# Second layer's experts: u and v rows in one table, one 8 KB gather per token and slot, weighted sum by a diagonal tile

## Chip, core and metric

The kernel runs on one core of a Trainium2 chip. The metric is the device time of one execution in microseconds (us), as the median of three runs. A core has a matrix engine (PE), a vector engine (DVE), a scalar engine (ACT), a general engine (POOL, GpSimd), which also writes the descriptors of indirect transfers, a queue engine (SP) for plain transfers, and 16 DMA engines that all transfers share.

## The reference

Two layers, each a token mixer followed by a feed-forward part with 16,384 small experts. Only the feed-forward part of the second layer is touched. It works on 256 tokens of width 1024, in two tiles of 128. For each token and each of 8 heads it picks 16 experts and adds their outputs:

```
q = (xb @ w_q).reshape(T, PEER_HEADS, 2, PEER_DQ // 2)
s = jnp.einsum('thpd,hpnd->thpn', q, keys).astype(jnp.float32)
s_top, i_top = lax.top_k(s, PEER_TOPK)
...
best, sel = lax.top_k(cand, PEER_TOPK)
eidx = jnp.take_along_axis(cidx, sel, axis=-1)
g = jax.nn.softmax(best, axis=-1)
act = jax.nn.gelu(jnp.einsum('td,thkd->thk', xb, u[eidx]).astype(jnp.float32))
return jnp.einsum('thk,thkd->td', (g * act).astype(v.dtype), v[eidx]).astype(h.dtype)
```

So each of the 256 tokens needs 128 rows of `u` and the same 128 rows of `v`, 4 KB each in fp32: 128 MB of `u` and 128 MB of `v` in all (268 million bytes). Nothing of it is reused, since every token has its own list. I call one pair (expert number 16h+k of each token of a tile) a slot: a tile has 128 slots, the layer 256.

## The kernel before

After the first layer and the second layer's mixer, `phase_norm` leaves the normed tokens in `hT` (a token per partition) and transposed in `hp`. Then `phase_stream` (L1817) does all of the experts' part, with a hand-written order on every engine and semaphores between them:

- **Scores.** PE runs 16 queries (`query`, L1972, 24 products of 128x256 each at L117 to L119, then `sub_scores`, L1927). ACT splits each weight slab in a high part (`w_hi`, L2011), DVE in a low part (`low`, L2101), and ACT copies query and scores out of PSUM (L2023, L2008).
- **Routing.** DVE runs `route` (L2080) once per tile and head, 16 times: the top 16 of both halves, of their sums, and the expert numbers, a chain of short instructions in which each waits for the one before.
- **u rows.** POOL gathers one row of `in_u_rows` per token for each slot (L1922, 128 rows of 4 KB, 512 KB in all). DVE multiplies it with `hT` and sums (`dot`, L2125, at L2132).
- **Weights.** After 64 slots of a tile (a unit `u`, 4 in all), ACT takes Exp and Gelu of 64 columns at once (L2034, L2039), DVE multiplies with the gates (`weights`), PE transposes expert numbers and weights (L1941, L1946), and DVE spreads the weights into `wdiag`, whose columns are mostly zero (`spread_weights`, L2149).
- **v rows.** Here a gather takes the 64 rows of each of two tokens (the transposed numbers `eidT`). Four such gathers make a `quad` (L1948): 8 products of 128x512 whose weights have 32 columns, four in each half going to four different groups of 32 output rows. So a quad reads 2 MB.

POOL's order is a list (`order`, L1836): the 64 `u` gathers of the first unit, then 4 `u` and 4 `v` gathers by turns, then 64 `v` gathers. All go through a ring of 18 buffers of 4 KB per partition; a gather waits until its buffer was consumed (`consumed`, L1854), by a dot or by a quad. DVE alternates in pieces of a head: a whole `route`, then the 16 dots of the head before, with up to three `low` between them. At the end `evac`, `turn_back` and `add_back` bring the sum of each tile back to `xT`, and `phase_norm` and one store end the program. The first layer's experts (`phase_mixed`) use gathers of 4 KB rows too, beside plain loads of the same tables by SP.

## Time and profile before

| | us |
|---|---|
| median of 3 runs (3319.77 to 3323.53) | 3321.89 |
| span of the profiled execution, first to last instruction | 3310.8 |
| outside the span, against the median | 11.1 |
| first gather of `phase_stream` issued | 2490.5 |
| last one issued | 3281.6 |
| last quad ends | 3289.2 |
| DVE's share of the span | 62% |
| PE's share of the span | 70% |

The profiled execution has no time of its own beside its span. The clock of PE that the hardware granted (PEclk in the views) is given as a share of 2.4 GHz: 1.00 is 2.4 GHz, 0.50 is 1.2 GHz, and a value between is a mean over a stretch with both. "DMA share" is the mean busy share of the 16 DMA engines, GB/s what they moved. A matmul in fp32 leaves two records; records that lie side by side are merged in the timeline, which gives the time from the first start to the last end.

### The profile page before, as it was taken

How to read it: one execution, taken by the hardware profiler on the slowest of the kernel's cores; microseconds unless marked ns; L12 is line 12 of the kernel's file. 1: busy time of each engine (PE TensorE's matmuls, PEld its weight loads, DVE VectorE, ACT ScalarE, POOL GpSimd, SP SyncE). 2: the span in 40 equal slices, each digit the busy share in tenths (PEclk: the TensorE clock that was granted, in tenths of full speed). 3: DMA queues.
4: the chain of work that ended last, by engine and by line, in shares of the span. 5: the costliest groups of instructions: out<-in, count | busy, mean ns of one | idle time of the engine just before them, and what ended most of it. 6: DMA issues, size and time to landing. Idle time of an engine off the chain costs nothing. (4 is left out here: it accounts for less than half of the span.)

```text
span 3310.8 us, 41079 instructions
## 1 busy us (share of the span) xinstructions
PE 2319.7 (70%) x15570; PEld 1772.9 (54%) x15570; DVE 2038.1 (62%) x4539; ACT 884.6 (27%) x1475; POOL 1445.0 (44%) x1270
## 2 busy tenths in 40 slices
PE   5977799794558787888899998887973423333345
PEld 3777555592357777777678775786553300000001
DVE  3576444499968898888543344665537956656530
ACT  3323144321363333333233333422431100000000
POOL 1034001330017675565655552022046677767764
PEclk8975698896789999999899999886876756565566
DMA  5210141134359999999999996210037799999997
GB/s 204 67 29 1 59 153 52 64 129 152 127 212 406 407 404 365 400 390 400 402 405 406 405 406 264 93 30 9 1 110 280 267 358 356 349 363 349 353 374 269
DMA packets 248756, 816.92 MB, mean 247 GB/s; under 512 B 26776, under 2 KB 45784, under 8 KB 247664
## 3 DMA queue, kind: packets, MB, share of 16 engines
q0 software_dynamic: 147456, 536.94, 42.3%
q1 hardware_dynamic: 101104, 277.35, 22.4%
q8 instruction: 125, 2.05, 0.3%
q14 instruction: 71, 0.58, 0.1%
HBM read 796.37 MB, written 17.83 MB: 246 GB/s over the span
## 5 line engine op out<-in xcount | busy, mean ns | idle before, releaser
L1960 PE MATMUL ps<-sparse_ring,sparse_wdiag 128*32 128x512 f32 x1024 | 225.7, 995 | 402.2 <-DMA sparse_ring<-in_v_rows,eidT 372.7
L2322 POOL DMA_INDIRECT sparse_ring<-in_v_rows,eidT x256 | 282.7, 1104 | 291.8 <-PE ps L2371 220.8
L2132 DVE CUSTOM_DVE_ANT_0 sparse_ring<-sparse_ring,hT 128x1024 f32<-128x1024 f32 x256 | 304.7, 1222 | 163.5 <-DMA sparse_ring<-in_u_rows,eid 159.2
L2322 POOL DMA_INDIRECT sparse_ring<-in_u_rows,eid x256 | 347.1, 1356 | 118.0 <-issue 68.1
L117 PE MATMUL ps<-h_hi,peer_uh 128*128 128x256 f32 x1024 | 310.3, 303 | 83.6 <-DVE peer_ul L2434 77.3
L1960 PEld LDWEIGHTS ps<-sparse_ring,sparse_wdiag 128*32 128x32 f32 x1024 | 44.4, 152 | 573.0 <-issue 573.0
L1922 POOL DMA_INDIRECT sparse_ring<-in_u_rows,eid x256 | 299.4, 1169 | 102.7 <-issue 75.9
L1922 POOL DMA_INDIRECT sparse_ring<-in_v_rows,eidT x256 | 280.8, 1097 | 123.4 <-issue 73.7
L2460 DVE CUSTOM_DVE_ANT_0 sparse_ring<-sparse_ring,hT 128x1024 f32<-128x1024 f32 x256 | 304.1, 1223 | 37.1 <-DMA sparse_ring<-in_u_rows,eid 34.9
L119 PE MATMUL ps<-h_hi,peer_ul 128*128 128x256 f32 x1024 | 299.0, 292 | 1.9 <-issue 1.9
L118 PE MATMUL ps<-h_lo,peer_uh 128*128 128x256 f32 x1024 | 299.6, 293 | 0.5 <-issue 0.4
L118 PE MATMUL ps<-peer_wl,peer_vh 128*128 128x256 f32 x1024 | 290.8, 284 | 2.6 <-issue 2.6
L119 PE MATMUL ps<-peer_wh,peer_vl 128*128 128x256 f32 x1024 | 290.4, 284 | 2.0 <-issue 1.9
L117 PE MATMUL ps<-peer_wh,peer_vh 128*128 128x256 f32 x1024 | 291.4, 285 | 0.3 <-issue 0.3
L117 PEld LDWEIGHTS ps<-h_hi,peer_uh 128*128 128x128 f32 x1024 | 206.1, 201 | 149.1 <-DVE peer_ul L2434 95.5
L2434 DVE TENSOR_TENSOR peer_ul<-peer_u,peer_uh 128x1024 fp32r<-128x1024 f32 x128 | 156.5, 1222 | 180.7 <-ACT peer_uh L2399 111.4
L2399 ACT ACTIVATE peer_uh<-peer_u 128x1024 fp32r<-128x1024 f32 x128 | 135.2, 1057 | 305.1 <-DMA peer_u<-in_uT 291.4
L119 PEld LDWEIGHTS ps<-h_hi,peer_ul 128*128 128x128 f32 x1024 | 206.2, 201 | 2.9 <-issue 2.9
L118 PEld LDWEIGHTS ps<-h_lo,peer_uh 128*128 128x128 f32 x1024 | 206.6, 202 | 0.8 <-issue 0.7
L117 PEld LDWEIGHTS ps<-peer_wh,peer_vh 128*128 128x128 f32 x1024 | 197.6, 193 | 4.7 <-issue 4.7
L119 PEld LDWEIGHTS ps<-peer_wh,peer_vl 128*128 128x128 f32 x1024 | 197.3, 193 | 2.9 <-issue 2.9
L118 PEld LDWEIGHTS ps<-peer_wl,peer_vh 128*128 128x128 f32 x1024 | 197.4, 193 | 1.7 <-issue 1.6
(410 smaller groups left out, 5385.4 us busy)
## 6 DMA issues: line engine op xcount, KB each, us to landing
peer_u<-in_uT SPq DMA_DIRECT2D x128, 512.0 KB
peer_v<-in_v_rows SPq DMA_DIRECT2D x128, 512.0 KB
ada_slab<-in_ada_w SPq DMA_DIRECT2D x20, 2048.0 KB, 8.6
proj_slab<-in_w_fm SPq DMA_DIRECT2D x38, 512.0 KB
route_slab<-in_w_pq SPq DMA_DIRECT2D x32, 512.0 KB, 3.3
peer_gates<-dense_stage SPq DMA_DIRECT2D x4, 4096.0 KB, 13.0
peer_gates<-peer_gates SPq DMA_DIRECT2D x32, 512.0 KB
out_slab<-in_w_out SPq DMA_DIRECT2D x16, 512.0 KB, 3.8
```

Source lines behind the costliest of these rows:

```text
L117: nc.tensor.matmul(out, w[0], x[0], start=start, stop=False)
L118: nc.tensor.matmul(out, w[0], x[1], start=False, stop=False)
L119: return nc.tensor.matmul(out, w[1], x[0], start=False, stop=stop)
L1922: nc.gpsimd.indirect_dma_start(out=ring[:, s % R], out_offset=None, in_=rows, in_offset=bass.IndirectOffsetOnAxis(ap=col, axis=0)).then_in ...
L1960: mm = nc.tensor.matmul(ps[32 * q:32 * (q + 1), 6 + half, :], wdiag[:, q, HQ * half_h + j, :], ring[:, s % R, half * BANK:(half + 1) * BAN ...
L2132: nc.vector.tensor_tensor_reduce(out=ring[:, s % R], in0=ring[:, s % R], in1=hT[:, t], scale=1.0, scalar=0.0, op0=ALU.mult, op1=ALU.add, a ...
L2322: nc.gpsimd.indirect_dma_start(out=ring[:, s % R], out_offset=None, in_=rows, in_offset=bass.IndirectOffsetOnAxis(ap=at, axis=0)).then_inc ...
L2399: nc.scalar.activation(uh[:, e % 2], us[:, e % SW], ACT.Copy).then_inc(uhi, 1)
L2434: nc.vector.tensor_tensor(ul[:, e % 2], us[:, e % SW], f32(uh[:, e % 2]), ALU.subtract).then_inc(ulo, 1)
L2460: nc.vector.tensor_tensor_reduce(out=ring[:, s % R], in0=ring[:, s % R], in1=hT[:, t], scale=1.0, scalar=0.0, op0=ALU.mult, op1=ALU.add, a ...
```

## The change

The two layers' tables are no longer one. The first layer reads `peer_u[0]` and `peer_v[0]` as before; for the second a table `in_uv_rows` holds the `u` row and the `v` row of an expert side by side, 8 KB. In `phase_stream`:

- POOL issues 256 gathers of 128 rows of 8 KB in place of 512 of 4 KB. The ring has 11 buffers of 8 KB per partition (88 KB, before 72 KB), and a buffer is free when the slot's product is done.
- The weighted sum is made per slot: `slot` multiplies the `v` half of the buffer by a 128x128 diagonal tile with the slot's weights, two products of 128x512, all 256 slots into four banks (two per tile). The transposes, `eidT` and `wdiag` go.
- ACT makes the weights for two slots at a time (`weights`): a Gelu of 2 columns, two scalings by the gate, and two diagonal tiles out of `ident`, of which there are 4 buffers. Exp and sum of a head are one instruction, 16 in all, and the gates another.
- DVE runs `dot` per slot on the `u` half, with two steps of a `route` (of 14) after each until all are done; the queries 5 to 15 are spread over the first 33 slots on PE, ACT and DVE (`query_at`).

The diff, cut to its core (the routing's instructions are the same, cut into steps by `yield`):

```diff
-            R = 18
+            S = nt * NS
+            R = 11
+            DG = 4
+            FIRST = 5
+            query_at = {(2 * i + 1 if i < 3 else 3 * i - 1): FIRST + i for i in range(HP + 1 - FIRST)}
...
-                ring = sb(st, f"sparse_ring{l}", [P, R, D_MODEL])
+                ring = sb(st, f"pair_ring{l}", [P, R, 2 * D_MODEL])
+                diag = sb(st, f"pair_diag{l}", [P, DG, P])
...
+                        for s in range(S):
                             if s >= R:
-                                pool.wait_ge(*consumed(s - R))
+                                pool.wait_ge(slot_mm, s - R + 1)
+                            if s % TOPK == 0:
+                                pool.wait_ge(eid_done, s // TOPK + 1)
+                            nc.gpsimd.indirect_dma_start(out=ring[:, s % R], out_offset=None, in_=d["uv_rows"],
+                                                         in_offset=bass.IndirectOffsetOnAxis(ap=eid[:, s:s + 1], axis=0))\
+                                .then_inc(row_in[s % R], 16)
...
+                        def slot(s):
+                            t, i = s // NS, s % NS
+                            pe.wait_ge(diag_done, s + 1)
+                            for half in range(2):
+                                mm = nc.tensor.matmul(ps[:, 4 + 2 * t + half, :], diag[:, s % DG, :],
+                                                      ring[:, s % R, D_MODEL + half * BANK:D_MODEL + (half + 1) * BANK],
+                                                      start=(i == 0), stop=(i == NS - 1))
+                            mm.then_inc(slot_mm, 1)
...
+                        for c in range(FIRST):
                             query(c)
+                        for s in range(S):
+                            slot(s)
+                            if query_at.get(s, HP) < HP:
+                                query(query_at[s])
+                            elif s in query_at:
+                                sub_scores(HP - 1)
...
+                        def weights(s):
+                            act.wait_ge(dot_done, s + 2)
+                            nc.scalar.activation(dots[:, s:s + 2], dots[:, s:s + 2], ACT.Gelu_apprx_tanh).then_inc(gelu_done, 1)
+                            act.wait_ge(gelu_done, s // 2 + 1)
+                            if s % TOPK == 0:
+                                act.wait_ge(gate_done, s // TOPK + 1)
+                            for x in (s, s + 1):
+                                nc.scalar.activation(dots[:, x:x + 1], dots[:, x:x + 1], ACT.Copy, scale=gate[:, x:x + 1]).then_inc(wt_done, 1)
+                            for x in (s, s + 1):
+                                act.wait_ge(wt_done, x + 1)
+                                if x >= DG:
+                                    act.wait_ge(slot_mm, x - DG + 1)
+                                nc.scalar.activation(diag[:, x % DG], ident[:], ACT.Copy, scale=dots[:, x:x + 1]).then_inc(diag_done, 1)
...
+                        for s in range(S):
+                            dot(s)
+                            next(routes, None)
+                            next(routes, None)
+                            if query_at.get(s, HP) < HP:
+                                low(query_at[s])
+                            if s % TOPK == 11 and s + TOPK < S:
+                                invert(s // TOPK + 1)
+                            if s == NS + 24:
+                                add_back(0)
...
-    a["u_rows"] = peer_u.reshape(-1, D_MODEL)
-    a["v_rows"] = peer_v.reshape(-1, D_MODEL)
+    a["u_rows"] = peer_u[0]
+    a["v_rows"] = peer_v[0]
+    a["uv_rows"] = np.concatenate([peer_u[1], peer_v[1]], axis=-1)
```

How the instructions stand now. On DVE, before, from the end of the second head's `route` on (ISA is the dot and the read of its sum):

```order
L2095 SCALAR_TENSOR_TENSOR route_ij<-route_ij 128x16
L2098 TENSOR_SCALAR eidf<-route_ij 128x16
L2099 TENSOR_SCALAR eid<-route_ij 128x16
L2132 ISA sparse_ring,sparse_dots<-sparse_ring,hT 128x1024
L2132 ISA sparse_dots 128x1
L2132 ISA sparse_ring,sparse_dots<-sparse_ring,hT 128x1024
```

and after the change, from the first dot on (L2103 is the dot, L2098 is `low`, L2038 to L2088 the steps of `route`):

```order
L2103 ISA pair_ring,pair_dots<-pair_ring,hT 128x1024
L2103 ISA pair_dots 128x1
L2038 MAX route_top<-route_s 128x8 x2
L2042 MAX_INDEX route_idx<-route_top,route_s 128x8 x2
L2043 MATCH_REPLACE route_s<-route_top,route_s 128x128 x2
L2103 ISA pair_ring,pair_dots<-pair_ring,hT 128x1024
L2103 ISA pair_dots 128x1
L2047 MAX route_top<-route_s 128x8 x2
L2051 MAX_INDEX route_idx<-route_top,route_s 128x8 x2
L2052 TENSOR_TENSOR route_cand<-route_top 128x256
L2098 TENSOR_TENSOR route_wl<-route_slab,route_wh 128x1024
```

A dot now stands after every second step, where sixteen stood in a row after a whole `route`. On PE, at the end of the stream, before (L1960 is the quads, L1941 and L1946 the transposes, L1969 `turn_back`):

```order
L1960 MATMUL ps<-sparse_ring,sparse_wdiag 32x512 x112
L1941 MATMUL ps<-ident,eid_twice 128x128
L1960 MATMUL ps<-sparse_ring,sparse_wdiag 32x512 x8
L1946 MATMUL ps<-ident,sparse_wt_twice 128x128
L1960 MATMUL ps<-sparse_ring,sparse_wdiag 32x512 x136
```

and after (L1919 is `slot`, L1928 `turn_back`):

```order
L1895 MATMUL ps<-route_keys,route_q 128x128 x2
L1919 MATMUL ps<-pair_ring,pair_diag 128x512 x6
L1895 MATMUL ps<-route_keys,route_q 128x128 x2
L1919 MATMUL ps<-pair_ring,pair_diag 128x512 x216
L1928 MATMUL ps<-ident,hT 128x128 x8
L1919 MATMUL ps<-pair_ring,pair_diag 128x512 x230
```

There are 512 products in both, now 128 rows wide and not 32. On ACT, which had 8 instructions for the weights of all four units beside 8 table loads, the same stretch is now, around the fifth pair of slots (L1955 `w_hi`, L1963 and L1948 the copies out of PSUM, L1983 Gelu, L1988 scaling, L1993 diagonal tile, L1973 Exp):

```order
L1955 ACTIVATE route_wh<-route_slab 128x1024
L1963 ACTIVATE route_q<-ps 128x256
L1948 ACTIVATE route_s<-ps 128x256
L1983 ACTIVATE pair_dots<-pair_dots 128x2
L1988 ACTIVATE pair_dots<-pair_dots,gate 128x1 x2
L1993 ACTIVATE pair_diag<-ident,pair_dots 128x128 x2
L1973 ACT_TABLE_LOAD
L1973 ACTIVATE route_best,route_esum<-route_best,route_nbest 128x16
L1983 ACT_TABLE_LOAD
L1983 ACTIVATE pair_dots<-pair_dots 128x2
```

Five instructions stand between the dots of a pair and its products, and an Exp with two table loads comes once per 16 slots.

## Rows read from the trace of the kernel before

**Rows 1.** The windows view: busy time of each engine in nine stretches.
```profile
core 0: us, PE busy (x) PEld busy (x) DVE busy (x) ACT busy (x) POOL busy (x), PEclk, DMA share, GB/s
2478.00:2492.00 14.00, 6.68 (x52) 6.28 (x51) 11.11 (x38) 4.07 (x8) 1.49 (x1) 0.91 0.12 39
2492.00:2496.00 4.00, 4.00 (x20) 4.00 (x20) 0.49 (x1) 0.00 (x0) 3.08 (x4) 0.50 0.94 281
2496.00:2516.00 20.00, 4.43 (x37) 4.24 (x35) 5.18 (x26) 3.32 (x6) 11.28 (x13) 0.67 1.00 399
2500.00:2640.00 140.00, 53.34 (x318) 50.52 (x317) 126.62 (x318) 22.43 (x40) 96.40 (x67) 0.69 0.79 281
2640.00:3200.00 560.00, 176.34 (x782) 35.39 (x782) 323.93 (x782) 9.04 (x13) 422.25 (x381) 0.58 0.96 356
3205.00:3270.00 65.00, 37.71 (x184) 7.97 (x184) 0.00 (x0) 0.00 (x0) 43.54 (x47) 0.70 0.97 374
1400.00:1500.00 100.00, 81.70 (x631) 73.09 (x630) 80.60 (x121) 33.15 (x49) 60.83 (x49) 0.91 1.01 393
1750.00:1950.00 200.00, 195.81 (x1610) 156.84 (x1612) 80.13 (x102) 69.62 (x103) 109.20 (x101) 1.00 1.03 406
1300.00:1900.00 600.00, 539.02 (x4222) 451.18 (x4220) 368.36 (x528) 198.92 (x294) 352.41 (x302) 0.95 1.02 401
```

**Rows 2.** Groups by line with shapes kept apart, from 2400 us to the end.
```profile
L1922 POOL DMA_INDIRECT sparse_ring<-in_u_rows,eid x256 | 299.4, 1169 | 102.7 <-issue 75.9 <-DVE eid L2099 26.3 <-remote 0.3
L1922 POOL DMA_INDIRECT sparse_ring<-in_v_rows,eidT x256 | 280.8, 1097 | 123.4 <-issue 73.7 <-remote 28.0 <-DVE eidT L2139 12.9
L1960 PE MATMUL ps<-sparse_ring,sparse_wdiag 128*32 128x512 f32 x1024 | 225.7, 995 | 402.2 <-DMA sparse_ring<-in_v_rows,eidT 372.7 <-issue 29.5
```

**Rows 3.** Timeline of POOL: start us, us, engine, line, operation, idle before it.
```profile
2490.51 1.77 POOL L1922 DMA_INDIRECT sparse_ring<-in_u_rows,eid  x1 [14.27 <-DVE eid L2099]
2492.58 0.94 POOL L1922 DMA_INDIRECT sparse_ring<-in_u_rows,eid  x1 [0.30 <-issue]
...
2526.00 1.98 POOL L1922 DMA_INDIRECT sparse_ring<-in_u_rows,eid  x1 [0.30 <-issue]
2528.28 1.99 POOL L1922 DMA_INDIRECT sparse_ring<-in_u_rows,eid  x1 [0.30 <-issue]
...
2543.26 0.94 POOL L1922 DMA_INDIRECT sparse_ring<-in_u_rows,eid  x1 [0.30 <-issue]
2544.50 0.94 POOL L1922 DMA_INDIRECT sparse_ring<-in_u_rows,eid  x1 [0.30 <-issue]
```

**Rows 4.** Timeline of DVE in the first heads.
```profile
2521.37 1.22 DVE L2132 CUSTOM_DVE_ANT_0 sparse_ring<-sparse_ring,hT 128x1024 f32<-128x1024 f32 x1
2522.52 1.22 DVE L2132 CUSTOM_DVE_ANT_0 sparse_ring<-sparse_ring,hT 128x1024 f32<-128x1024 f32 x1
...
2540.82 0.48 DVE L2066 MAX8 route_top<-route_s 128x8 f32<-128x128 f32 x2
...
2549.47 1.22 DVE L2132 CUSTOM_DVE_ANT_0 sparse_ring<-sparse_ring,hT 128x1024 f32<-128x1024 f32 x1
```

**Rows 5.** Timeline of PE: two quads, then a square fp32 product with 512 columns.
```profile
3140.39 3.64 PE L1960 MATMUL ps<-sparse_ring,sparse_wdiag 128*32 128x512 f32 x16 [11.61 <-DMA sparse_ring<-in_v_rows,eidT]
...
3287.28 1.92 PE L1960 MATMUL ps<-sparse_ring,sparse_wdiag 128*32 128x512 f32 x16 [1.31 <-DMA sparse_ring<-in_v_rows,eidT]
...
27.65 1.88 PE L297 MATMUL ps<-hk,meanD 128*128 128x512 f32 x4
```

**Rows 6.** Timeline of PE in the first queries, and one product of scores.
```profile
2473.33 0.41 PE L119 MATMUL ps<-h_hi,route_wl 128*128 128x256 f32 x1
2473.54 0.41 PE L117 MATMUL ps<-h_hi,route_wh 128*128 128x256 f32 x1
...
2479.06 0.28 PE L119 MATMUL ps<-h_hi,route_wl 128*128 128x256 f32 x1
2479.18 0.28 PE L117 MATMUL ps<-h_hi,route_wh 128*128 128x256 f32 x1
...
2499.82 0.61 PE L1933 MATMUL ps<-route_keys,route_q 128*128 128x128 f32 x4
```

**Rows 7.** Groups of ACT in the whole program, shapes kept apart.
```profile
L1782 ACT ACTIVATE hot_j<-iota,dense_nj 128x128 f32<-128x128 f32 x102 | 31.5, 389 | 12.6 <-DVE dense_nj L1753 12.6
L943 ACT ACTIVATE scan_xq<-cum 128x128 f32<-128x128 f32 x15 | 3.6, 296 | 0.0
L2034 ACT ACT_TABLE_LOAD x4 | 5.1, 1283 | 0.1
L2015 ACT ACTIVATE route_wh<-route_slab 128x1024 fp32r<-128x1024 f32 x14 | 14.8, 1057 | 111.3 <-PE ps L119 89.4 <-issue 13.5 <-remote 8.4
L2023 ACT ACTIVATE route_q<-ps 128x256 f32<-128x256 f32 x16 | 5.9, 369 | 21.0 <-PE ps L119 21.0
L1136 ACT ACTIVATE lame<-lame 128x2 f32<-128x2 f32 x2 | 0.4, 204 | 10.6 <-DVE lame L1280 10.6
```

**Rows 8.** What L1922 and L1960 do: ns min/median/max, first and last start.
```profile
L1922 POOL DMA_INDIRECT sparse_ring<-in_u_rows,eid x256: 934/941/2007, 2490.5 to 3181.9; - x128
L1922 POOL DMA_INDIRECT sparse_ring<-in_v_rows,eidT x256: 932/941/1989, 2632.8 to 3281.6; - x128
...
L1960 PE MATMUL ps<-sparse_ring,sparse_wdiag x1024: 589/1061/1064, 2643.0 to 3288.6; 128*32 128x512 f32 x171
```
**Rows 9.** The waits view, 2640 to 3290: total us, times, longest.
```profile
PE ps L1960 <- DMA sparse_ring<-in_v_rows,eidT: 372.7, 56, 12.9
```

More of the change, by code:

```diff
@@ L21 @@
 from contextlib import ExitStack
+import itertools
 import math
@@ L1861, in phase_stream @@
+            (dot_done, gelu_done, wt_done, diag_done, slot_mm, acc_ev, tr_mm) = (
+                sem(f"stream_{x}{l}") for x in ("dot", "gelu", "wt", "diag", "slot_mm", "acc_ev", "tr_mm"))
             with ExitStack() as st:
@@ L2047, in _ @@
+                        queried(1)
+                        queried(2)
                         exps(0)
-                        gelu(0)
-                        exps(1)
-                        gelu(1)
-                        exps(2)
-                        gelu(2)
-                        evac(0)
-                        exps(3)
-                        gelu(3)
+                        queried(3)
+                        gates(0)
+                        queried(4)
+                        for s in range(0, S, 2):
+                            weights(s)
+                            for x in (s - 2, s - 1):
+                                if query_at.get(x, HP) < HP:
+                                    queried(query_at[x])
+                                elif x in query_at:
+                                    s_copy(HP - 1)
+                            if s % TOPK == 8 and s + TOPK < S:
+                                exps(s // TOPK + 1)
+                            if s % TOPK == 12 and s + TOPK < S:
+                                gates(s // TOPK + 1)
+                            if s == NS + 4:
+                                evac(0)
@@ L2125, in dot @@
-                        def dot(t, h, between=()):
-                            for i in range(TOPK * h, TOPK * (h + 1)):
-                                if i % TOPK in (5, 10, 15) and len(between) >= i % TOPK // 5:
-                                    low(between[i % TOPK // 5 - 1])
-                                s = at["u", t, i]
-                                dve.wait_ge(row_in[s % R], 16 * (s // R + 1))
-                                nc.vector.tensor_tensor_reduce(
-                                    out=ring[:, s % R], in0=ring[:, s % R], in1=hT[:, t], scale=1.0, scalar=0.0,
-                                    op0=ALU.mult, op1=ALU.add, accum_out=dots[:, t, i:i + 1]).then_inc(dot_done, 1)
@@ L2149, in spread_weights, with dot @@
-                        def spread_weights(u):
-                            dve.wait_ge(wt_mm, u + 1)
-                            dve.wait_ge(diag_cleared, 1)
-                            if u >= 2:
-                                dve.wait_ge(quad_mm, HQ * (u - 1))
-                            nc.vector.tensor_copy(diag(u % 2, 0), of_token(ps[:, 4, P:2 * P], 0))
-                            nc.vector.tensor_copy(diag(u % 2, 1), of_token(ps[:, 4, P:2 * P], 1)).then_inc(spread, 1)
+                        def dot(s):
+                            dve.wait_ge(row_in[s % R], 16 * (s // R + 1))
+                            row = ring[:, s % R, 0:D_MODEL]
+                            nc.vector.tensor_tensor_reduce(out=row, in0=row, in1=hT[:, s // NS], scale=1.0, scalar=0.0,
+                                                           op0=ALU.mult, op1=ALU.add, accum_out=dots[:, s:s + 1]).then_inc(dot_done, 1)
@@ L2194, in _ @@
-                        last = 2 * nt - 1
-                        dot(nt - 1, PH - 1)
-                        close(last)
-                        weights(last)
-                        add_back(0)
-                        spread_weights(last)
+                        low(2)
+                        for _ in route(0):
+                            pass
+                        low(3)
+                        low(4)
+                        invert(0)
+                        routes = itertools.chain.from_iterable(route(j) for j in range(1, nt * PH))
@@ new lines, in _ @@
+                        for s in range(S):
[8 more added lines that the diff above has]
+                                add_back(0)
+                        for _ in routes:
+                            pass
```

299 lines of the change are left out of this document (97 added, 202 removed).

## Prediction, made before the change was run

> **What bounds the kernel now.** I read the windows view first, then the groups by line, then timelines. The first layer is untouched, so only what runs from 2490.5 us on counts. From 2640 to 3200 the DMA engines look full: share 0.96, 356 GB/s [rows 1]. That tempts one to say that the stream is bound by memory, and that moving the same 268 MB in larger pieces changes nothing. Two other rows of the same view speak against it: the same gathers, alone, moved 399 GB/s from 2496 to 2516, when sixteen of them were issued in a row, and the first layer's stretch holds 401 GB/s for 600 us, two gathers in three transfers among it [rows 1].
>
> What is full is POOL. It was busy for 422.25 us of these 560, with 381 gathers: 1.11 us each. In front of each the timeline shows 0.30 us of idle time put down to "issue" [rows 3], so 381 x 1.41 = 537 us, 96% of the stretch. The timeline also tells why a gather costs 1.11: 0.94 us where DVE does short routing steps or nothing, 1.98 us where DVE runs its dots back to back [rows 3, 4]. At 2.29 us for 512 KB POOL feeds 229 GB/s, at 1.24 us 423 GB/s. I read the DMA share of 0.96 as packets that take longer because little is queued behind them. From 3205 to 3270, with DVE idle, the rate rises to 374 GB/s [rows 1].
>
> Before 2640 it is DVE that is full: 126.62 us of 140, at 281 GB/s [rows 1]. One head costs 30 us there: 8.65 us of `route` (from 2540.82 to 2549.47), 16 dots and up to 3 `low` at 1.15 us each [rows 4]. PE waits for its `v` rows most of the time: 402.2 us of idle time before L1960, 372.7 of it by DMA [rows 2].
>
> **The change, part by part.**
>
> POOL. 512 gathers become 256. If the cost is one per row descriptor, each still has 128 rows, so 0.94 to 1.99 us plus 0.30: 1.24 to 2.29 us per MB, where before it was 2.5 to 4.6. That is below every other term here. If a row of 8 KB costs two descriptors, it is twice 0.94 to 1.99 and one 0.30: with dots for 40% of the time, 2 x 1.36 + 0.30 = 3.0 us. No gather of 8 KB rows is in this trace. I take the first, the nearest row, and keep 3.0 as a rival.
>
> DMA. 1,048,576 bytes per slot. At 401 GB/s, the rate held over 600 us with two queues, this is 2.61 us; at 410 it would be 2.56, at 356, the rate of this stream now, 2.95. I take 2.61.
>
> PE. This is the price of the change. A quad has 8 products in four groups of 32 output columns that run side by side: its 16 records take 3.64 us at one time and 1.92 us at another [rows 5]. A slot has only 2 products, but 128 wide, so nothing runs beside them: the record pitch of the square product at L297 is (1.88 - 0.59)/3 = 0.43 us, 4 records 1.72 us [rows 5]; at half the clock 3.44 us. So a slot costs PE about what a quad does, and there are 256 instead of 64. In all 440 us at 2.4 GHz or 881 us at 1.2 GHz, for a stream that lasts some 680 us. The queries add 11 x (24 x 0.12 + 0.61) = 38 us [rows 6], at half the clock the 24 take 0.21 each.
>
> Which clock is granted? Now, with PE idle for two thirds of the stretch, 0.58; with 37.71 us busy of 65, 0.70; with 82 of 100 busy, 0.91; with 98% busy, 1.00 [rows 1]. In rows 6 the queries begin at 0.21 us each and go on at 0.12 without a gap between them. A slot needs 1.72 of 2.61 us at full clock, 66%, and more than all of it at half, so at the low clock PE never idles, and in rows 6 the work without idle time is what raised the clock. I expect a mean near 0.8, 2.15 us per slot. The Trainium skill warns of the contrary in "TensorE: Matmul & The Clock Gate", section "HAM oscillation — how this bites in real kernels": bursts of matmuls shorter than the wait for data between them start slow each time. What this would give is the third rival.
>
> DVE. Per slot a dot, 1.15, and two of 14 steps of a route, 2 x 8.65/14 = 1.24: 2.39 us, under 2.61. In the first 33 slots 11 `low` add 0.38. The routes end after 15 x 14/2 = 105 slots; from there it is 1.15 to 1.3. Steps that waited for their forerunner now have a dot in between.
>
> ACT. Per pair of slots a Gelu of 2 columns, two scalings, two tiles: 3 x 0.20 + 2 x 0.39 = 1.4 us (0.30 to 0.39 for a tile, by its two nearest rows) of 5.2 us [rows 7]. It is on no path by its sum, but it stands in each slot's. Behind it on ACT stand `w_hi`, 1.06, and the copies, 0.37, for which DVE's `low` and PE's query wait. 15 heads bring two table loads, 2 x 1.28, each: in front of a pair, and not in sum.
>
> The ring. A buffer is held from its issue until its product. I add: 2.1 for POOL at most, 5.7 from issue to landing (the last gather starts at 3281.6, the last quad at 3287.28 [rows 5, 8]), a dot that waits and one that runs, 3.6, the pair's partner, 2.6, ACT 1.4, PE up to 3.4: 19 us, with the table loads 21. Eleven buffers at 2.61 us are 28.7 us. The ring isn't the bound; at the low clock on PE it nearly is.
>
> **The sum.** The first gather starts when it did, at 2490.5: what comes ahead of it (five queries, the first route) is as before. The second has landed near 2500 (5.7 us after its issue, 1.3 for the larger size), a dot, 1.2, and ACT's Gelu, scalings and first tile with a table load, some 2.7 us, to 2504, follow, and PE can begin slot 0 at 2505. The first 33 slots: PE's own work is 33 x 1.72 + 38 = 95 us at full clock, DVE's 33 x 2.77 = 91 us, DMA's 86. These hold each other up (a query waits for `low`, `low` for `w_hi`, and that for the query two before), so I take PE's at a clock of 0.9: 106 us, to 2611. By then the ring is full, about 40 slots have landed, and 216 are to come: 216 x 2.61 = 564 us, to 3175. The last pair's dots, ACT and two slots on PE take 7 us: 3182. Before, the last quad ended at 3289.2, and what follows (`evac`, `turn_back`, `add_back`, final norm) is unchanged. That is 107 us less. I give back 8 us for dips in the DMA share at the table loads and `turn_back(0)`: 99 us less, a span of 3211.8. The median of the runs was 11.1 us above the span, so **3223 us**.
>
> **The rivals.**
>
> 1. *Memory is the bound already.* If rows taken at random cannot come faster than the 356 GB/s of now, a slot takes 2.95 us: 2611 + 216 x 2.95 + 7 = 3255, 34 us less, 3288. For it: the DMA share of 0.96. Against it: the 399 GB/s of the same gathers. The Trainium skill takes this side: "DMA: Bandwidth & Descriptors", section "Where 436 GB/s comes from", has about 358 GB/s for a core's share of HBM as what binds; this trace disagrees, with 401 GB/s over 600 us. Chance 0.12.
> 2. *POOL stays the bound.* Two descriptors for a row, 3.0 us per slot: 2611 + 648 + 7 = 3266, 23 us less, 3299. Chance 0.08.
> 3. *PE becomes the bound, and the kernel is slower.* If the clock stays at 1.2 GHz through the stream, as it mostly does now, the stream lasts 256 x 3.44 + 11 x (24 x 0.21 + 1.2) = 949 us from 2505 on, to 3454: 165 us more, 3487. It decides from the clock at which a slot takes more than 3.1 us, (3289 - 2611 - 7)/216, which is 0.55 of full. For it: 0.58 granted in the stream now. Against it: that is with 56 waits for DMA of up to 12.9 us [rows 9], and no row shows a PE without idle time that stayed slow. Chance 0.10.
> 4. *The chain per slot is longer than I add up*: a wait between POOL, DVE, ACT and PE in the first 33 slots costs 40 us more, or the ring runs short in the routes. About 3263. Chance 0.12.
>
> My forecast has 0.58.
>
> **How the numbers follow.** The likeliest case by itself reaches from 3200 (410 GB/s and no dips: 107 + 11 less, 3204; a little for a faster start) to 3250. The range takes in rivals 1, 2 and 4, so 3195 to 3300, and leaves out rival 3 and what lies beyond it. A measurement of this kernel tells 0.2% from no change, 6.6 us. Faster by more than that: the forecast and rivals 1, 2 and 4, less a little for mixed cases, 0.87. Within it 0.03, slower 0.10.
>
> **What would show it.** Right: gathers near or above 400 GB/s after slot 33, POOL idle for a third of the time or more with about 256 spans of 1 to 2 us, PEclk above 0.75 in the stream, and idle time of PE before its slots put down to ACT's tile, and of ACT's Gelu to dots that wait for DMA. The first 33 slots would end near 2611. Wrong: PE busy for over 95% with PEclk near 0.5 (rival 3), POOL's spans above 2.2 us on average (rival 2), a DMA share of 1 at 360 GB/s with POOL idle (rival 1), or gathers that wait for PE's `slot_mm` while the DMA engines are below 0.9 (rival 4).

## The result, and the profile after

The changed kernel takes **3185.05 us** (median of four runs, 3183.18 to 3187.82) where the kernel before takes 3320.83 on the same chip (four runs, 3309.5 to 3323.53): a ratio of 0.9600, 95% interval 0.9583 to 0.9618. The prediction had 3223 us with a range from 3195 to 3300: right in direction, but the range did not hold the result, which lies 10 us under its lower end. The profiled execution has a span of 3181.7 us and a time of 3183.49; its span is 129.1 us shorter than that of before.

The windows view of the kernel after, its columns as in [rows 1]:

```profile
2496.00:2516.00 20.00, 8.47 (x45) 6.73 (x44) 8.01 (x28) 5.95 (x13) 7.38 (x8) 0.67 1.01 422
2520.00:2540.00 20.00, 20.00 (x103) 13.83 (x102) 17.49 (x51) 9.88 (x27) 6.36 (x7) 1.00 1.01 417
2580.00:2600.00 20.00, 18.07 (x79) 11.74 (x79) 13.92 (x40) 9.10 (x25) 8.96 (x6) 0.91 0.94 380
2600.00:2640.00 40.00, 39.28 (x115) 19.11 (x114) 39.53 (x126) 16.82 (x57) 26.16 (x21) 1.00 0.97 384
2640.00:3120.00 480.00, 358.66 (x776) 139.85 (x774) 293.95 (x667) 159.92 (x540) 189.66 (x193) 0.99 1.01 421
```

The DMA engines, at 281 GB/s up to 2640 and 356 from there on before [rows 1], now move 417 to 422 GB/s but for one dip around 2600, where PE is busy for 18.07 of 20 us and then for 39.28 of 40. POOL is busy for 40% of the long stretch, PE for 75% of it, at a granted clock of 0.99.

The groups by line, as in [rows 2]:

```profile
L1919 PE MATMUL ps<-pair_ring,pair_diag 128*128 128x512 f32 x1024 | 476.3, 610 | 144.8 <-ACT pair_diag L1993 142.2 <-issue 2.6
L2103 DVE CUSTOM_DVE_ANT_0 pair_ring<-pair_ring,hT 128x1024 f32<-128x1024 f32 x256 | 312.9, 1222 | 206.7 <-DMA pair_ring<-in_uv_rows,eid 206.7
L1883 POOL DMA_INDIRECT pair_ring<-in_uv_rows,eid x256 | 268.2, 1048 | 391.9 <-PE ps L1919 364.0 <-DVE eid L2088 17.8 <-issue 10.2
L1993 ACT ACTIVATE pair_diag<-ident,pair_dots 128x128 f32<-128x128 f32 x256 | 87.4, 387 | 2.0 <-PE ps L1919 1.7
```

Read the third row against POOL's two in [rows 2]: 512 gathers and 580 us have become 256 and 268, and the idle time in front of a gather is no longer "issue" but a wait for PE, which frees the buffer. A gather of 8 KB rows costs POOL what one of 4 KB rows costs, 0.94 us with little beside it. PE waits for ACT's diagonal tiles, ACT for the dots, and DVE's dots for landings. So the transfers bind, and each engine waits for them in its turn.

The timeline of POOL where the ring first fills, and in the middle of the stream (columns as in [rows 3]):

```profile
2502.10 0.94 POOL L1883 DMA_INDIRECT pair_ring<-in_uv_rows,eid  x1 [0.30 <-issue]
2503.34 0.94 POOL L1883 DMA_INDIRECT pair_ring<-in_uv_rows,eid  x1 [0.30 <-issue]
...
2804.45 0.94 POOL L1883 DMA_INDIRECT pair_ring<-in_uv_rows,eid  x1 [0.78 <-PE ps L1919]
2807.70 0.94 POOL L1883 DMA_INDIRECT pair_ring<-in_uv_rows,eid  x1 [2.31 <-PE ps L1919]
```

and DVE's, there, a dot every 2.49 us:

```profile
2815.54 1.22 DVE L2103 CUSTOM_DVE_ANT_0 pair_ring<-pair_ring,hT 128x1024 f32<-128x1024 f32 x1 [1.25 <-DMA pair_ring<-in_uv_rows,eid]
2816.69 0.08 DVE L2103 DVE_READ_ACCUMULATOR2_ANT pair_dots<- 128x1 f32 x1
2818.03 1.23 DVE L2103 CUSTOM_DVE_ANT_0 pair_ring<-pair_ring,hT 128x1024 f32<-128x1024 f32 x1 [1.26 <-DMA pair_ring<-in_uv_rows,eid]
```

I paired the k-th gather with the k-th dot over the whole stream. From slot 60 on, a dot begins some 20 us after POOL was done with its gather (17.8 to 21.1): eight transfers of 2.49 us stand in front of it. This *lead* of POOL over the dots tells most of what follows.

### The profile page after: what moved, and what is told of

Its sections match the earlier page's. It is cut to its first block and busy times, and to the rows that moved or that the text cites. A ratio compares the mean times of both kernels' runs of the same rounds, so it can differ in the third digit from the quotient of the medians.

```text
span 3181.7 us, 41584 instructions
## 1 busy us (share of the span) xinstructions
PE 2546.1 (80%) x15562; PEld 1903.4 (60%) x15562; DVE 2022.4 (64%) x4495; ACT 1084.4 (34%) x2179; POOL 1119.1 (35%) x1013
## 5 line engine op out<-in xcount | busy, mean ns | idle before, releaser
L1919 PE MATMUL ps<-pair_ring,pair_diag 128*128 128x512 f32 x1024 | 476.3, 610 | 144.8 <-ACT pair_diag L1993 142.2
L2103 DVE CUSTOM_DVE_ANT_0 pair_ring<-pair_ring,hT 128x1024 f32<-128x1024 f32 x256 | 312.9, 1222 | 206.7 <-DMA pair_ring<-in_uv_rows,eid 206.7
L1919 PEld LDWEIGHTS ps<-pair_ring,pair_diag 128*128 128x128 f32 x1024 | 187.1, 192 | 423.3 <-ACT pair_diag L1993 228.5
L1883 POOL DMA_INDIRECT pair_ring<-in_uv_rows,eid x256 | 268.2, 1048 | 391.9 <-PE ps L1919 364.0
L2251 POOL DMA_INDIRECT sparse_ring<-in_v_rows,eidT x256 | 279.5, 1092 | 298.4 <-PE ps L2300 226.9
L2251 POOL DMA_INDIRECT sparse_ring<-in_u_rows,eid x256 | 339.4, 1326 | 122.5 <-issue 68.1
L2389 DVE CUSTOM_DVE_ANT_0 sparse_ring<-sparse_ring,hT 128x1024 f32<-128x1024 f32 x256 | 304.7, 1224 | 41.9 <-DMA sparse_ring<-in_u_rows,eid 35.7
L2300 PE MATMUL ps<-sparse_ring,sparse_wdiag 128*32 128x512 f32 x1024 | 137.2, 653 | 67.2 <-DMA sparse_ring<-in_v_rows,eidT 66.2
```

What stands on the lines that cost most here:

```text
L1883: nc.gpsimd.indirect_dma_start(out=ring[:, s % R], out_offset=None, in_=d["uv_rows"], in_offset=bass.IndirectOffsetOnAxis(ap=eid[:, s:s + ...
L1919: mm = nc.tensor.matmul(ps[:, 4 + 2 * t + half, :], diag[:, s % DG, :], ring[:, s % R, D_MODEL + half * BANK:D_MODEL + (half + 1) * BANK], ...
L2103: nc.vector.tensor_tensor_reduce(out=row, in0=row, in1=hT[:, s // NS], scale=1.0, scalar=0.0, op0=ALU.mult, op1=ALU.add, accum_out=dots[:, ...
L2251: nc.gpsimd.indirect_dma_start(out=ring[:, s % R], out_offset=None, in_=rows, in_offset=bass.IndirectOffsetOnAxis(ap=at, axis=0)).then_inc ...
L2300: mm = nc.tensor.matmul(ps[32 * q:32 * (q + 1), 6 + half, :], wdiag[:, q, j, :], ring[:, s % R, half * BANK:(half + 1) * BANK], start=(j = ...
L2389: nc.vector.tensor_tensor_reduce(out=ring[:, s % R], in0=ring[:, s % R], in1=hT[:, t], scale=1.0, scalar=0.0, op0=ALU.mult, op1=ALU.add, a ...
```

## The experiments

Sixteen runs, made in five groups. Each group has its own runs of before on its chip (medians 3316 to 3330 us), so kernels of different groups are compared by their ratios to before. After's own program came to 3185.05 and 3185.19 us on two occasions, but to ratios of 0.9600 and 0.9566, since before moved: a difference of under some 10 us is not told by the ratios.

### Is POOL's issue the bound that was removed?

**Two gathers of 4 KB per slot**, the rest as after:

```diff
-nc.gpsimd.indirect_dma_start(out=ring[:, s % R], out_offset=None, in_=d["uv_rows"],
+for half, table in enumerate(("u1_rows", "v1_rows")):
+    nc.gpsimd.indirect_dma_start(out=ring[:, s % R, half * D_MODEL:(half + 1) * D_MODEL], out_offset=None, in_=d[table],
...
-dve.wait_ge(row_in[s % R], 16 * (s // R + 1))
+dve.wait_ge(row_in[s % R], 32 * (s // R + 1))
```

> After's program, with the 8 KB gather of a slot issued as two gathers of 4 KB, the u row from one table and the v row from another, into the two halves of the same ring buffer: 512 gathers, all else as in after. Theory A (before's second stream was bound by GpSimd's issue of its gathers, 1.11 us of work and 0.30 us of issue each, and after has half as many of them): GpSimd needs 2 x 1.41 = 2.8 us per slot, more than the DMA engines' 2.49 in after, the stream grows by 256 x 0.3 = 80 us, and the time comes to 3255 to 3285 us, with GpSimd's idle time no longer waits on TensorE. Rival (what after gains it gains by larger packets alone): the DMA engines would need 2.54 us per slot by 4 KB packets of 159 ns each on 16 engines, the time comes to about 3198, and GpSimd still waits for buffers.

Measured: 3285.89 us, ratio 0.9869 (0.9838 to 0.9900), 101 us above after, 1 us beyond theory A's upper end. The windows view (columns as above) and POOL's timeline:

```profile
2720.00:3120.00 400.00, 281.99 (x567) 111.12 (x566) 211.53 (x475) 119.07 (x397) 299.75 (x277) 0.90 0.96 362
```

```profile
2798.34 2.08 POOL L1884 DMA_INDIRECT pair_ring<-in_u_rows,eid  x1 [0.30 <-issue]
2800.73 0.94 POOL L1884 DMA_INDIRECT pair_ring<-in_v_rows,eid  x1 [0.31 <-issue]
2801.98 0.94 POOL L1884 DMA_INDIRECT pair_ring<-in_u_rows,eid  x1 [0.30 <-issue]
2803.22 1.68 POOL L1884 DMA_INDIRECT pair_ring<-in_v_rows,eid  x1 [0.31 <-issue]
```

From 2720 to 3120 POOL is busy for 299.75 us with 277 gathers, and with 0.3 us in front of each, 96% of the time is gone. It leads the dots by 5.1 us in the later slots, so little stands in the queue. This also splits the gain. The new order of the work (slots in place of heads and quads, with twice as many gathers as after) gives 1.3% of the time; the rest, some 3% or 101 us, needs the single gather.

**Control**, after's program again: 

> After's program unchanged, on the same chip as the other runs of this call: 3185 us within 5.

3185.19 us (3180.77 to 3188.13), ratio 0.9566.

**Short dots**, in after, in the split version and in before:

```diff
-row = ring[:, s % R, 0:D_MODEL]
+row = ring[:, s % R, 0:P]
...
```

> After's program with the dot product over the first 128 of the 1024 columns (the rest of each dot is left out), the control for the short dots. If after's stream is bound by the DMA engines alone, the time is within 15 us of after's 3185 (the stretch where the routes and the dots share VectorE may lose its small gaps, 5 to 10 us). If VectorE's 1.2 us per slot lay on the path of every slot, it would be 50 us and more faster.

3183.96 us. DVE's 1.2 us per slot is on no path in after.

> Before's program, with the dot product of its second stream over the first 128 of the 1024 columns (the rest of each dot is left out). Theory A (before's stream waits for GpSimd, whose gathers are slowed from 0.94 to as much as 1.98 us by VectorE's work beside them): a gather falls to 0.94 + 0.30 us, the DMA engines' 1.27 us per gather by 4 KB packets of 159 ns becomes the bound, and the stream of 381 gathers from 2640 on shrinks from 560 us to about 485, so the time falls by 60 to 100 us, to 3220 to 3260. Rival (before's stream is bound by the DMA engines already, at the 4 KB rows' rate): no change beyond 15 us.

3277.68 us, ratio 0.9855 (0.9830 to 0.9880), some 50 us less: gathers of 0.94 us in the mean in place of 1.11 make before faster, as the theory has it, but by less than its 60 to 100. The DMA engines moved 370 GB/s from 2640 to 3200, and POOL, busy for 371.99 us of these 560 with 395 gathers and 0.3 us in front of each, was at 88%.

> As the run with two gathers per slot, and the dot product of a slot runs over the first 128 of the 1024 columns only (the rest of each dot is left out), so VectorE's long operations, beside which a gather took 1.98 us instead of 0.94, are gone. Theory A: GpSimd needs 2 x 1.24 = 2.48 us per slot, just under the DMA engines' 2.54, and the time falls to 3190 to 3215. Rival (the number of packets or the DMA of 4 KB rows itself limits a split stream, and GpSimd's speed beside VectorE has no part): the time stays at that of the run with the whole dots.

3274.03 us: of 101 us the short dots gave back 12, where theory A had some 80. So either the 4 KB rows bind once POOL is relieved, or something else comes with 512 gathers. The next group was made to tell these apart.

### The number of gathers, or the size of the rows?

**Two gathers of 64 rows of 8 KB** (the first half of the partitions, then the second):

```diff
+for p, c in ((0, s), (P // 2, s ^ 1)):
+    nc.gpsimd.indirect_dma_start(out=ring[p:p + P // 2, s % R], out_offset=None, in_=d["uv_rows"],
+                                 in_offset=bass.IndirectOffsetOnAxis(ap=eid[0:P // 2, c:c + 1], axis=0))\
...
```

> After's program, with each slot's gather issued as two gathers of 64 rows of 8 KB, into the two halves of the partitions (the second takes the first 64 indices of the neighbouring slot, so half the rows are other tokens' and the sum is another one). The number of gathers is that of the run with split rows (512), the packets are those of after (8 KB each). Theory B (the run with split rows lost its 101 us to the 4 KB packets, of which the DMA engines took 359 GB/s at a busy share of 0.96, as before's): packets of 8 KB go at 421 GB/s again, and the time is within 20 us of after's 3185, unless GpSimd's 2 x (0.94 + 0.30) to 2 x (1.14 + 0.30) = 2.5 to 2.9 us per slot bind, which a smaller gather should make shorter. Theory C (the number of gathers, GpSimd's instructions and the landings' signals, sets the rate): the time is that of the run with split rows, 3286.

Four runs far apart, 3548, 3566, 3708 and 3738 us; by the two fastest the ratio is 1.0705 (1.0662 to 1.0748), some 370 us above after, and neither theory had it. The profile is of the slowest of them. The windows view:

```profile
2720.00:3120.00 400.00, 248.60 (x344) 94.90 (x343) 171.68 (x484) 70.66 (x242) 176.75 (x172) 0.74 1.02 227
```

The DMA engines are full, at 227 GB/s. Their 8 KB packets take 586 ns in the mean, where after's take 314. So gathers into half of the partitions ran at little over half the rate in this execution. The fastest was 190 us shorter; if all of that lies in the stream, whose 268 MB took some 1217 us here, it moved about 260 GB/s (an estimate). The run also shows that POOL's price is hardly one per row: 0.90 us for 64 rows, 0.94 for 128. The question stayed open.

**A small second gather beside the 8 KB one** (128 bytes per row; the ring has 10 buffers here and in its two variants below, to make room):

```diff
+nc.gpsimd.indirect_dma_start(out=tiny[:, s % R], out_offset=None, in_=d["tiny_rows"],
+                             in_offset=bass.IndirectOffsetOnAxis(ap=eid[:, s:s + 1], axis=0))\
+    .then_inc(row_in[s % R], 16)
...
```

> After's program with a second gather per slot, of 128 rows of 128 bytes from a small table, which nothing reads (and 10 buffers in the ring in place of 11, to make room): 512 gathers and twice the packets, while the rows that matter still come in packets of 8 KB. Theory B (the size of the packets that carry the rows sets the rate): the 8 KB packets stay at 314 ns with hardly one above 400, and GpSimd, at 2 x (0.94 + 0.30) = 2.5 to 2 x (1.05 + 0.30) = 2.7 us per slot, now binds by a little: 3185 to 3245 us. Theory C (twice as many gathers and packets is what slows the engines, whatever their size): the 8 KB packets show slow ones as the 4 KB ones did (some 4% of 600 ns), GpSimd has waits for the queue, and the time comes near the 3286 of the run with split rows.

3271.71 us, ratio 0.9862 (0.9841 to 0.9883), which is the split version's 0.9869, though the rows come in 8 KB pieces and only 1.6% more bytes are moved. POOL's timeline again shows gathers without a pause:

```profile
2800.59 1.26 POOL L1884 DMA_INDIRECT pair_ring<-in_uv_rows,eid  x1 [0.30 <-issue]
2802.16 1.05 POOL L1887 DMA_INDIRECT tiny<-in_tiny_rows,eid  x1 [0.30 <-issue]
2803.51 0.94 POOL L1884 DMA_INDIRECT pair_ring<-in_uv_rows,eid  x1 [0.30 <-issue]
2804.75 1.54 POOL L1887 DMA_INDIRECT tiny<-in_tiny_rows,eid  x1 [0.31 <-issue]
```

and the windows view:

```profile
2720.00:3120.00 400.00, 285.84 (x572) 111.88 (x570) 212.02 (x471) 119.68 (x400) 300.35 (x284) 0.92 0.98 376
```

284 gathers, 300.35 us and 0.3 in front of each: 96%. The lead over the dots is 3.6 us at the end, and still the windows view has a DMA share of 0.98. The packets explain it. The usual 8 KB packet takes 309 ns, but 8% of them far longer, mostly up to 0.9 us, so that the mean is 338; in after, where the queue is long, 0.1% are slow. *A share near 1 does not mean that the engines bind*: a packet's time in the trace can hold a wait. The plainest case is the version with all products twice, further below. There PE binds, POOL issues no more gathers than in after, and the DMA engines move 305 GB/s; yet their share is 0.89, and 16% of the 8 KB packets take over 0.4 us. So slow packets come with engines that are fed too little, and need no second gather. Of the expectation's two theories the result is nearer to C's, but its reading, that the gathers slow the engines, has no support.

**The same with short dots**, and **with the small gather in every second ten slots** (`if s // R % 2:` ahead of it):

> The run with a small second gather (8 KB rows, 512 gathers), with the dots over the first 128 of the 1024 columns (the rest of each dot is left out), so that GpSimd issues at 1.24 us per gather. It stands to that run as the run with split rows and short dots (3274) stands to the one with split rows (3286). Theory E (the number of gathers, by GpSimd's issue and by stalls that come with it, whatever the rows' size): 3255 to 3275, with idle time of TensorE of 50 to 110 us put down to issue, as in the other runs with 512 gathers. Rival F (with GpSimd relieved it was the 4 KB packets that bound the other run): 8 KB rows flow at 2.49 to 2.6 us per slot, 3185 to 3215.

3273.59 us, ratio 0.9855 (0.9809 to 0.9902), as the split version with short dots, and 2 us above the same with whole dots. Theory E: the size of the rows is not what these streams are short of.

> The run with a small second gather, in which only every second ten slots have it: 384 gathers. GpSimd then needs 1.5 x 1.36 = 2.0 us per slot, under the transfers' 2.49, and in ten slots with two gathers falls behind by 10 x 0.35 = 3.5 us, which the ring covers. Theory A (GpSimd's issue is a bound, which costs nothing while it is lower than another): 3185 to 3195. Rival (each further gather costs a share of the 87 us by slowing the packets around it, 0.34 us apiece): 3185 + 128 x 0.34 = 3229.

3199.85 us, ratio 0.9639 (0.9592 to 0.9685). 126 further gathers cost 15 us, which the ratios cannot tell from nothing, and 256 cost 87. The cost does not grow in proportion, which would give 3229, but sets in late, as with a bound, if a soft one: theory A, with 5 us more than it allowed.

**Split rows with 6 buffers**:

> The run with split rows (two gathers of 4 KB per slot), with 6 buffers in the ring in place of 11, so that at most 12 gathers of 4 KB are under way, and GpSimd meets the ring's limit before that of the queue. Theory D (the slow packets, 4.5% of the 4 KB packets at some 600 ns, come from a full queue, of which GpSimd's waits of up to 4.8 us for none of the program's engines speak): they become fewer, and the time falls from 3286 or stays, though 6 buffers alone cost 13 us. Rival (they belong to a stream of 4 KB packets at any depth): the slow packets stay at 4 to 5%, and the time is 3286 to 3310.

3286.81 us, ratio 0.9898, with as many slow packets as with 11 buffers (some 4.5% of them in both, mean 173 ns from 2720 to 3120). A full queue is not their cause: theory D falls, and its rival came true.

What stays open is why relieving POOL gave back so little, 12 us with split rows and nothing with the small gather. With short dots it issues every 1.24 us, 2.49 per slot, just what the transfers take, so it can make up for no delay. And delays there are, in the waits view of the split version with short dots, from 2720 to 3120:

```profile
PE ps L1920 <- issue: 107.7, 30, 9.2
...
POOL pair_ring L1884 <- remote: 34.2, 13, 4.9
```

In each of the five kernels with two gathers per slot into all partitions, PE sits idle for 62 to 108 us of this stretch for nothing that the waits view names; in after it is 2.6. POOL's longer waits, all eleven of them from 2720 to 2900, stand in front of the first gather of a slot, where it waits for a buffer that PE holds. The timeline says more. Here is one of these pauses:

```profile
2758.22 0.18 DVE L2076 CAST route_self<-route_sela 128x32 f32<-128x32 uint32 x1 [3.96 <-issue]
...
2766.03 0.40 ACT L1994 ACTIVATE pair_diag<-ident,pair_dots 128x128 f32<-128x128 f32 x1 [8.06 <-issue]
...
2766.49 3.78 PE L1920 MATMUL ps<-pair_ring,pair_diag 128*128 128x512 f32 x4 [6.48 <-issue]
```

PE starts when ACT's diagonal tile is done, and so it is with every such pause of PE of over 1 us in these five kernels (27 here, 105.6 of the 107.7 us): "issue" stands for a wait for ACT's tile. ACT and DVE pause as well. The step of a route at 2758.22 waits only for DVE's own step before it, and comes 3.96 us after that one. Pauses of over 1 us in front of such steps come 11 times in this stretch, 2 to 15 times in the other four, 22 times in before's, and not once in after's. So something delays several engines at once in streams where POOL issues nearly without a pause. Its cause was not found, and what part of the 87 to 101 us it has, no run tells.

### The rest of the sum

**Products twice**, and **one product in place of two**:

```diff
-for half in range(2):
+for n_mm, half in enumerate((0, 1, 0, 1)):
```
```diff
-for half in range(2):
+for half in range(2 if i in (0, NS - 1) else 1):
```

> After's program with the two products of each slot done twice, so that the experts' sum counts double. TensorE then needs 4 x 0.61 = 2.4 us per slot at the full clock by 610 ns each of after's row (before's quads: 3.64 us at the lower level for what is here one slot's two products, 1.92 at the higher). If a product's 610 ns are pure work, the stream sits at the edge of TensorE and the DMA engines, 2.4 to 2.5 us per slot, and the time grows by 0 to 30 us; if the duration read off the trace hides part of its price (1.72 us for two products, as the prediction had it, so 3.44 for four), TensorE is the bound and the time grows by 220 to 250 us.

3459.79 us (one run), 275 more, where the second reading of the expectation had 220 to 250; PE without a pause:

```profile
2720.00:3120.00 400.00, 400.00 (x940) 177.53 (x939) 192.95 (x485) 104.17 (x330) 131.34 (x117) 1.00 0.89 305
```

940 records at 8 per slot are 117.5 slots in 400 us, 3.40 us each: 0.425 us per record, 1.70 for a slot of after, where the prediction had 1.72 from the record pitch in [rows 5]. The mean of one record in a group (610 ns) is no price, since records overlap.

> After's program with the product of the first 512 columns alone in all slots but the first and the last of a tile (the second half of the columns of the sum is left out for them). TensorE's busy share in the stream falls from 74% to about 37%. If the clock follows the duty of the stream, as the prediction took it from before's 1.2 GHz quads, the granted clock in the stretch from 2700 to 3100 falls clearly under 1.00; the time stays within 10 us of after's, since the DMA engines bind. Rival (with gaps of 2 us or less the clock stays up at any duty): 1.00 throughout.

3181.68 us (one run): the time of after. The windows view:

```profile
2720.00:3120.00 400.00, 231.69 (x335) 73.50 (x333) 222.87 (x443) 134.08 (x452) 162.72 (x161) 0.78 1.01 421
```

The granted clock of the stretch is 0.78, so part of it ran at 1.2 GHz, and it costs nothing, since PE has time. PE is busy for 58%, where the expectation had 37, with idle stretches of up to 3.9 us. In after, from 2640 to 3120, with 75% busy and idle stretches of up to 2.3 us, it is 0.99.

**Shorter rings**, `R = 8` and `R = 6`:

> After's program with 8 buffers in the ring in place of 11. By the prediction's own sum a buffer is held 19 to 21 us from issue to release, and 8 buffers give 8 x 2.49 = 19.9 us: the edge, 0 to 15 us slower. Rival (in after's trace 9 to 11 gathers stand issued and not landed at any time from 2650 on, so that a buffer's time is mostly queueing, and what it needs is far less): within 5 us of 3185.

> After's program with 6 buffers. By the prediction's hold of 19 to 21 us per buffer each slot would cost 20 / 6 = 3.3 us, and the time would grow by some 200 us. Rival (queueing makes most of the hold): within 15 us of 3185, the difference lying between 2560 and 2700, where VectorE is full and fewer buffers cover fewer of its delays.

3189.71 and 3198.05 us, 5 and 13 more than after; the ratios, 0.9600 (0.9570 to 0.9630) and 0.9625 (0.9595 to 0.9656), do not tell either from after. The 200 us that a hold of 20 us would cost with 6 buffers did not come. A buffer is not needed for 20 us: it stands in the queue for most of them. With 6 buffers POOL leads the dots by 7.3 us, and the rate is still 418 GB/s.

**Whole routes** ahead of a head's 16 dots, in place of two steps behind each dot:

> After's program with the 14 steps of each later route written whole ahead of the 16 dots of its head, in place of two steps behind each dot. Theory (the interleaving lets the dots run at the transfers' rate while the routes go on): each route is then 14 steps in a row, about 19 us in which no buffer is dotted, and the 11 buffers of the ring hold 27 us of transfers at 2.49 us per slot, of which some 19 to 21 are needed by a slot's own hold: the DMA engines run dry in each of the later heads of the routes, and the time grows by 20 to 60 us. Rival (the ring is deep enough to cover a route): under 5 us.

3192.65 us, 8 more (ratio 0.9593, 0.9564 to 0.9622), between the theory's 20 to 60 and the rival's 5: the ring covers most of a route. From 2720 to 3120 the granted clock is 0.91, and PE has idle stretches of up to 6.6 us.

**Fewer steps behind a dot** in the later heads, to relieve DVE around 2600:

```diff
-next(routes, None)
+if s < TOPK:
+    next(routes, None)
```

> After's program with two steps of the later routes behind each of the first 16 dots, and one behind each dot from there on in place of two, so that VectorE has 1.2 + 0.6 us of work per slot where it has 2.4. In after's trace the DMA engines fall to 380 and 384 GB/s from 2580 to 2640, where VectorE is full. If those dips are VectorE's, they go, and 2 to 5 us with them; but the second tile's routes and the indices end later (they need 14 slots of 16 per head and stay ahead of the gathers by one head only), so that GpSimd's waits for indices may take the place of them: 0 to 60 us slower. The likelier by a little is a gain of up to 5 us, which is the width of the measurement.

3188.14 us (3183.39 to 3192.56), a ratio of 0.9595 (0.9573 to 0.9617), that of after: no gain. The windows view of 2600 to 2620, in after and here:

```profile
2600.00:2620.00 20.00, 20.00 (x71) 10.99 (x70) 19.74 (x61) 7.31 (x27) 11.23 (x9) 1.00 0.92 345
2600.00:2620.00 20.00, 20.00 (x71) 10.99 (x70) 16.51 (x44) 8.35 (x33) 10.09 (x9) 1.00 0.95 349
```

DVE is relieved, and the dip of this window stays, with PE busy for all 20 us in both. So it is PE, with the last of the queries between its slots, that is full there, and not DVE alone. (From 2580 to 2600 the rate does rise, from 380 to 421 GB/s, without a gain in time.) No version that computes the whole sum beat the changed kernel.

## Where the prediction was right, and the term that failed

*POOL's issue was before's bound*: held for the number of gathers, in part for POOL's time. The price rows of its step, 1.11 + 0.30 us per gather and 96% of the stretch, come back in the runs with 512 gathers at full dots (1.08 and 1.06 us in the first two, 96%), and the step from 512 to 256 is worth 87 to 101 us. But where POOL's time per gather alone was cut, by short dots, it gave 50 us in before, of 60 to 100, and 12 and none in the two versions with 512 gathers and the new order, of some 80. That POOL's time is all that the second gather costs is argued, not shown; the pauses of the other engines are the open rest.

*"I read the DMA share of 0.96 as packets that take longer because little is queued behind them"*: this fits what the runs show. In before's stream, too, the usual 4 KB packet takes 159 ns and the mean is 175. The next step forgot it.

*"At 401 GB/s, the rate held over 600 us with two queues, this is 2.61 us"*: **this is the term that failed**, in size. The slots come every 2.49 us. I took the rate from a stretch that two queues and other waits shared, and for the better end went no further than 410. Before's usual packet, 159 ns for 4 KB, is 412 GB/s over 16 engines, or 2.54 us per slot (an estimate), so about half of the miss could have been read there; the other half came with the larger rows, whose usual packet of 312 ns takes less than two of 159. The dots tell what it was worth: slot 40's begins at 2617.45, slot 255's at 3152.90, so 215 slots take 535 us where 2.61 each make 561: 26 us.

*The first 33 slots, 106 us, 40 landed by 2611*: right within 4 us, since 40 slots and the wait for the next one came to 2614, and the dot stands at 2617.45. The reasons were partly wrong, so that some of this is luck: PE began slot 0 at 2512.9, not 2505, but at a granted clock of 1.00 from 2520 to 2540, with no idle time, and the transfers were near their full rate from 2496 on.

*The last pair, 7 us*: 6.0, from the last dot at 3152.90 to the end of PE's last product at 3158.9.

*8 us for dips*: the dip at 2580 to 2640 lies inside the 4 us above, and there was none later. With 26 us from the rate and 8 from here, less 4, the span comes out 30 us under the 3211.8 forecast: 3181.7. The forecast of the time was 38 us too high, these 30 and most of the 9 of the next point. The 26 of the rate decide: with the transfers at 2.49 us the forecast would have been 3197, 12 us from the result, and a range built around it would have held it.

*11.1 us outside the span*: wrong by 9. Each run that has both numbers shows 1.8 us (3183.49 against 3181.7). Before's profiled execution was one of its fastest, if the same 1.8 us hold for it (3312.6, an estimate): its runs go from 3309.5 to 3323.5 on one chip.

*PE's granted clock near 0.8*: it was 0.99. The slot's price at full clock, 1.72 us, was right (1.70). The warning that I cited from the Trainium skill ("TensorE: Matmul & The Clock Gate", section "HAM oscillation — how this bites in real kernels") did not come true in after's stream. With one product per slot it did in part, by the granted clock of 0.78 in the stretch, and cost no time.

*The ring, 19 to 21 us per buffer*: too long for what a buffer needs, and too short for how long it is held when the queue is full, since the lead alone is 20 us then. Six buffers are nearly enough.

The rivals. Memory as the bound at 356 GB/s (0.12) fell with 421. The Trainium skill's 358 GB/s per core ("DMA: Bandwidth & Descriptors", section "Where 436 GB/s comes from") is exceeded here by 18%; the 435 GB/s that it gives for the ports into SBUF lies 3% above what after's stream reaches. POOL as the bound (0.08): a gather of 8 KB rows costs it what one of 4 KB rows does, 0.94 us; a price per row is not the reason, since 64 rows cost 0.90. PE at 1.2 GHz and slower (0.10): in the stream it never came near. A longer chain in the first slots (0.12): 8 us late at slot 0, and caught up.

## What to carry to other kernels

Where an engine issues gathers one by one, count them: time per gather with the idle time in front of it, against the time of its bytes; merging two tables so that one index fetches both rows halved that at no cost in transfer. Take a transfer's price from the usual duration of a packet of its size (309 ns for 8 KB, 424 GB/s over 16 engines) and not from the mean of a stretch or from a DMA share near 1, both of which hold waits. To see who binds, look at what the issuer waits for and at how long before its use each transfer was issued. In after, POOL waited for free buffers and led by 20 us of the 27 that its ring allows; in the two streams that POOL bound it had 0.3 us between gathers and led by 4 to 5. A short lead alone does not tell: with 6 buffers it was 7.3 us, at 418 GB/s.

## What the hardware showed beyond expectation

- Gathers into 64 of the 128 partitions ran at 227 GB/s in place of 421 in the profiled execution (the fastest of four at about 260, an estimate), with packets of 586 ns in place of 314. The Trainium skill has a reason that fits, in "DMA: Bandwidth & Descriptors", section "The descriptor swizzle": in a transfer to 128 partitions each engine writes through a port of its own, which belongs to certain partitions. That two engines share a port in a transfer to 64 is my conclusion, which no run shows by itself.
- POOL needs 0.90 us for a gather of 64 rows, 0.94 for 128 rows of 4 KB or of 8 KB, and up to 2.08 beside DVE's dots in the middle of the streams; the longest of after, 3.07 at 2549.81, stood beside a `low` and a dot.
- In streams where POOL issued gathers nearly without a pause, steps of DVE that wait for DVE's own step before them came up to 4.5 us late; in after's stream none came over 1 us late.
- Random rows of 8 KB from HBM came at 421 GB/s for 480 us, on one core.
